# PEER expert stage: one gather of paired U and V rows (32 tokens x 4 slots), with streamed weight tables, in a hybrid decoder layer

## The chip, the cores and the metric

The kernel runs on one core of a Trainium2 chip. The metric is the device time of one execution in microseconds (us); lower is better. Before the change three runs gave 4285.42, 4292.56 and 4297.67 us, so the median is 4292.56 us.

## What is computed

One decoder layer over 1024 tokens of width 1024, all in float32. First two token mixers (a gated linear attention, GLA, and an RG-LRU) are computed from one projection, merged by gates, and projected by `w_out`. Then comes the PEER expert stage, the long part. For each token and each of 8 heads it picks 16 of 16384 experts through a product of two key sets, so each token has 128 expert slots:

```
qry = (xt @ w_query).reshape(T, 8, 2, 128)
sub_scores = einsum('thpd,hpnd->thpn', qry, sub_keys)      # 2 x 128 scores a head
top_s, top_i = top_k(sub_scores, 16)
cand_s, cand_i = all 256 sums of a pair of top_s, and their expert numbers
best_s, best_pos = top_k(cand_s, 16); gates = softmax(best_s)
u_sel = u_table[expert_idx]; v_sel = v_table[expert_idx]    # rows of 1024 floats, 4 KB
act = gelu(einsum('td,thkd->thk', xt, u_sel))
out = einsum('thk,thkd->td', gates * act, v_sel)
```

With 1024 tokens x 128 slots there are 131,072 rows of U and as many of V, 4 KB each: 1073.7 MB in all. Norms, modulation vectors and a residual stand around both halves of the layer.

## The kernel before

Three stages follow one another, each one block of five engine programs: `conditioning_and_lru`, `gated_linear_attention`, `peer_block`. SyncE (SP) issues most direct DMAs, GpSimd (POOL) issues the gathers, TensorE (PE) multiplies, VectorE (DVE) and ScalarE (ACT) do the rest. Engines meet at semaphores; each engine's queue is strictly in order.

In the LRU stage, ACT, PE, DVE, POOL and SP each run a loop of 8 blocks (`j`), in GLA a loop of 4 heads (`h`). SP loads 512 KB weight tiles a few steps ahead in both.

`peer_block` handles the tokens in 8 tiles of 128, one token in each partition. Before the first tile, 16 products of keys and query weights make the table `Wk` (8 MB, kept in SBUF, as is `w_out`, 4 MB). A tile has 8 heads, a head 2 groups `G` of `R = 8` slots. For a slot POOL issues one gather of 128 U rows (`gather_u`, L1010, 8 buffers `ur`) and one of 128 V rows (`gather_v`, L1015, 4 buffers `vr`), each 512 KB, alternating in `both`. At the head of a group POOL also copies the indices twice (L1003). DVE multiplies a U buffer with the tokens' h2 and sums to one number a token (`products`, L1323), then forms the group's 8 gelu-and-gate coefficients with one tanh on ACT (L1329 to L1334, L1071). ACT builds for each slot a 128x128 diagonal matrix of coefficients (L1075). PE multiplies it with the V buffer into the accumulator `ps_acc` (L1178: two products of 512 columns, each shown as two MATMUL rows). Selection of a head's experts (`select_sides`, `select_pairs`, L1279 to L1316) is written into the same DVE program two heads ahead, so that gathers start once two heads of tile 0 are selected. A gather waits until its buffer is free: U for DVE (`u_used`), V for PE (`v_used`).

Of the kernel before, what the change touches and what calls it, by code (L numbers as in the profile page):

```python
# [30 lines left out]
SLOTS = PH * TOPK  # L31
NEG = -3.0e38
# [33 lines left out]

def conditioning_and_lru(nc, ctx, keep, a, mod_dram, merged_dram):


    hh, hl, alow, ident = keep["hh"], keep["hl"], keep["alow"], keep["ident"]  # L70
    Q = 256
    CQ = Q // P
    MOD1 = 2 * D // Q
    with ExitStack() as scope:
# [140 lines left out]
        def _(act):  # L215
# [36 lines left out]
            with act.Fori(0, KC) as j:  # L252
                act.wait_ge(projected[0], j + 1)
# [210 lines left out]
def gated_linear_attention(nc, ctx, keep, a, merged_dram):  # L464
# [6 lines left out]
    with ExitStack() as scope:  # L471
        def sb(name, shape, dt=F32):
            return scope.enter_context(nc.sbuf_tensor(name, shape, dt))

        def sem(name):
            return ctx.enter_context(nc.semaphore(name))
# [135 lines left out]

# [164 lines left out]
        def _(dve):  # L777
# [84 lines left out]
            step.end(HEADS)  # L862


def peer_block(nc, ctx, keep, a, mod_dram, merged_dram, out):
# [4 lines left out]
    R = 8  # L870
    GROUPS = TOPK // R
    VR = ND = 4
    with ExitStack() as scope:
# [11 lines left out]
        Wk = sb("Wk", [P, KC, 2 * PH * NK])  # L885
        w_out = sb("w_out", [P, KC, D])
        mod = sb("mod", [P, 4 * D])
        mT = sb("mT", [P, KC, P])
        x2n, x2c = sb("x2n", [P, D]), sb("x2c", [P, D])
        h2n, h2c = sb("h2n", [P, D]), sb("h2c", [P, D])  # L890
        h2T = sb("h2T", [P, KC, P])
        yf = sb("yf", [P, D])
        ur, vr = sb("ur", [P, R, D]), sb("vr", [P, VR, D])
        diag = sb("diag", [P, ND, P])
        zero = sb("zero", [P, P], mybir.dt.bfloat16)
        idx = sb("idx", [P, 2 * SLOTS], U32)
        gates = sb("gates", [P, 2 * SLOTS])
        uidx, vidx = sb("uidx", [P, 2, R], U32), sb("vidx", [P, 2, R], U32)
# [21 lines left out]
        const, small_in = sem("consts3"), sem("small_in3")  # L920
        wout_in = [sem("wout_in0"), sem("wout_in1")]
        wq_in = [sem(f"wq_in{i}") for i in range(4)]
        wk_done, wk_out = sem("wk_done"), sem("wk_out")
        mod_ready = sem("mod_ready")
        x_in, m_in = sem("x_in3"), sem("m_in")
        y_done, y_sq, y_root, y_rstd, y_used = sem("y_done"), sem("y_sq"), sem("y_root"), sem("y_rstd"), sem("y_used")
        x2_ready, h2_ready, h2_turned, h2T_out = sem("x2_ready"), sem("h2_ready"), sem("h2_turned"), sem("h2T_out")
        x2_copied, h2_copied = sem("x2_copied"), sem("h2_copied")
        sc_done, sc_used = sem("sc_done"), sem("sc_used")
        negm_ready, ex_out, sel_ready = sem("negm_ready"), sem("ex_out"), sem("sel_ready")  # L930
        ucopy, vcopy, pool_go = sem("ucopy"), sem("vcopy"), keep["go"]
        u_in = [sem(f"u_in{r}") for r in range(R)]
        v_in = [sem(f"v_in{r}") for r in range(VR)]
        u_used, v_used = sem("u_used"), sem("v_used")
        gel_ready, tanh_out, coef_ready, diag_out = sem("gel_ready"), sem("tanh_out"), sem("coef_ready"), sem("diag_out")
        acc_done, acc_out, f_root, f_rstd, f_ready, out_done = (sem(n) for n in ("acc_done", "acc_out", "f_root", "f_rstd", "f_ready", "out_done"))
        dve_step, dve_go = sem("dve_step3"), keep["go"]
# [4 lines left out]

        def group_at(G):

            return bass.ds(G % (2 * SLOTS // R) * R, R)

        @block.sync
        def _(sp):
            def load_keys(g, i):

                sp.dma_start(vr[:, i], a["wqT"][g].rearrange("o p d -> (o p) d")).then_inc(wq_in[i], 16)
                sp.dma_start(diag[:, i], a["keysT"][g].rearrange("o p d -> (o p) d")).then_inc(wq_in[i], 16)

            def merged_tile(t):
                sp.dma_start(mT[:], merged_dram[:, :, bass.ds(t * P, P)]).then_inc(m_in, 16)

            def x_tile(t):
                sp.dma_start(x2n[:], a["x"][bass.ds(t, 1)].rearrange("o p d -> (o p) d")).then_inc(x_in, 16)

            def store_tile(t):  # L960
                sp.wait_ge(f_ready, t + 1)
                sp.dma_start(out[bass.ds(t, 1)].rearrange("o p d -> (o p) d"), yf[:]).then_inc(out_done, 16)

            for s in range(2):
                load_keys(slice(s, s + 1), s)
            merged_tile(0)
            for s in range(2):
                sp.dma_start(w_out[:, :, s * HALF:(s + 1) * HALF], a["w_out"][:, :, s * HALF:(s + 1) * HALF]).then_inc(wout_in[s], 16)
            x_tile(0)
            sp.dma_start(mod[:], mod_dram).then_inc(small_in, 16)  # L970

            for i, n in enumerate(("gain_post_mix", "gain_pre_ffn", "gain_post_ffn")):
                sp.dma_start(ur[:, 2 + i], a[n].broadcast_to([P, D])).then_inc(small_in, 16)
            for i in range(2, 4):
                load_keys(slice(i, i + 1), i)
            with sp.Fori(0, PH // 2 - 1) as g:
                for i in range(4):
                    sp.wait_ge(wk_done, 4 * g + i + 1)
                    load_keys(bass.ds(4 * g + i + 4, 1), i)
            sp.wait_ge(y_done, 2)  # L980
            merged_tile(1)
# [12 lines left out]
        @block.gpsimd
        def _(pool):
            nc.gpsimd.memset(eps[:], EPS).then_inc(const, 1)
            nc.gpsimd.memset(zero[:], 0.0).then_inc(const, 1)
            nc.gpsimd.iota(iota[:], [[1, TOPK]], base=0, channel_multiplier=0, allow_small_or_imprecise_dtypes=True).then_inc(const, 1)

            def copy_indices(G, par, to, copied):  # L1000

                pool.sem_inc(pool_go, 1)
                nc.gpsimd.tensor_copy(to[:, par], idx[:, group_at(G)]).then_inc(copied, 1)  # L1003
                pool.wait_ge(copied, G + 1)

            def gather_u(G, par, r, first=False):
                if not first:
                    pool.wait_ge(u_used, R * (G - 1) + r + 1)  # L1008
                pool.sem_inc(pool_go, 1)
                pool.indirect_dma_start(ur[:, r], None, a["u"], bass.IndirectOffsetOnAxis(ap=uidx[:, par, r:r + 1], axis=0)).then_inc(u_in[r], 16)  # L1010

            def gather_v(G, par, r):
                pool.wait_ge(v_used, R * G + r + 1)
                pool.sem_inc(pool_go, 1)
                pool.indirect_dma_start(vr[:, r % VR], None, a["v"], bass.IndirectOffsetOnAxis(ap=vidx[:, par, r:r + 1], axis=0)).then_inc(v_in[r % VR], 16)  # L1015

            def both(G, par):

                copy_indices(G + 1, 1 - par, uidx, ucopy)
                copy_indices(G, par, vidx, vcopy)  # L1020
                for r in range(R):
                    gather_u(G + 1, 1 - par, r)
                    gather_v(G, par, r)

            pool.wait_ge(mod_ready, 1)
            pool.wait_ge(sel_ready, 1)
            copy_indices(0, 0, uidx, ucopy)
            for r in range(R):
                gather_u(0, 0, r, first=True)
            pool.wait_ge(wk_done, 2 * PH)  # L1030
            with pool.Fori(0, TC * PH - 1) as H:
                both(2 * H, 0)
                pool.wait_ge(sel_ready, H + 2)
                both(2 * H + 1, 1)
            last = 2 * TC * PH - 1
            both(last - 1, 0)
            copy_indices(last, 1, vidx, vcopy)
            for r in range(R):
                gather_v(last, 1, r)

        @block.scalar
        def _(act):
            S = nc.scalar
            act.wait_ge(const, 3)
            act.sem_inc(diag_out, R)

            def mixer_norm(t, stored):
                act.wait_ge(y_done, 2 * t + 2)
                if stored is not None:
# [11 lines left out]
            def tile_turned(t):  # L1061
# [3 lines left out]
            def select_gates(n):  # L1065
                act.wait_ge(negm_ready, n + 1)
# [75 lines left out]
        def _(pe):  # L1142
# [61 lines left out]
            for h in range(2):  # L1204
                scores(h, 0, h)
# [257 lines left out]
```

## Time and profile before

| | |
|---|---|
| median of 3 runs | 4292.56 us |
| span of the profiled execution, first to last instruction | 4370.2 us |
| PE, DVE, ACT, POOL busy | 76%, 58%, 22%, 61% |
| DMA moved | 1184.53 MB, mean 271 GB/s |
| software queue (POOL's gathers above all) | 1084.36 MB |

The profile gives the profiled execution's time as its span alone; it is 77.6 us above the median of the unprofiled runs. Busy shares are averages over three unlike stages: the mixers take about the first 926 us, the expert stage the rest. "DMA share" is the mean busy share of the core's 16 DMA engines.

### The profile page before, as it was taken

How to read it: one execution, taken by the hardware profiler on the slowest of the kernel's cores; microseconds unless marked ns; L12 is line 12 of the kernel's file. 1: busy time of each engine (PE TensorE's matmuls, PEld its weight loads, DVE VectorE, ACT ScalarE, POOL GpSimd, SP SyncE). 2: the span in 40 equal slices, each digit the busy share in tenths (PEclk: the TensorE clock that was granted, in tenths of full speed). 3: DMA queues.
4: the chain of work that ended last, by engine and by line, in shares of the span. 5: the costliest groups of instructions: out<-in, count | busy, mean ns of one | idle time of the engine just before them, and what ended most of it. 6: DMA issues, size and time to landing. Idle time of an engine off the chain costs nothing.

```text
span 4370.2 us, 44073 instructions
## 1 busy us (share of the span) xinstructions
PE 3333.3 (76%) x9929; PEld 1731.2 (40%) x9944; DVE 2548.4 (58%) x5725; ACT 961.4 (22%) x1993; POOL 2665.9 (61%) x2467
## 2 busy tenths in 40 slices
PE   6998999977777767777677677767777677777676
PEld 5775888854222322232233222323332233222232
DVE  5786656635555565556655655565556556555654
ACT  4232444432111111112111111111111111111111
POOL 2233322205777677767776777777777767777776
PEclk9999999989999999999999999999999999999998
DMA  4323111138889898989989999999998889898998
GB/s 178 133 100 116 43 58 58 38 135 288 320 320 329 318 327 317 331 315 327 323 318 325 326 331 322 326 326 339 317 330 318 314 320 330 319 324 319 332 339 293
DMA packets 334937, 1184.53 MB, mean 271 GB/s; under 512 B 36944, under 2 KB 51728, under 8 KB 330640
## 3 DMA queue, kind: packets, MB, share of 16 engines
q0 software_dynamic: 297984, 1084.36, 69.2%
q1 hardware_dynamic: 36880, 99.45, 6.3%
q14 instruction: 58, 0.48, 0.0%
q8 instruction: 15, 0.25, 0.0%
HBM read 1168.98 MB, written 14.68 MB: 271 GB/s over the span
## 4 chain that ended last, share of the span: by engine, by line
issue 23%; DMA 19%; POOL 19%; PE 14%; DVE 2%; POOLq 1%; ACT 1%; another core or an unknown queue 0%; SPq 0%; DVEq 0%; ACTq 0%
DMA vr<-in_v,vidx 16%; PE ps_acc L1178 10%; POOL vr L1015 9%; POOL ur L1010 8%; DMA ur<-in_u,uidx 2%; PE ps_y L1149 2%; PE ps_sc L1164 2%; DVE ur L1323 1%; POOL vidx L1003 1%; POOL uidx L1003 1%; DMA ur<-in_gain_post_ffn 0%; POOLq L1003 0%; PE ps_acc L1194 0%; POOLq L1008 0%
## 5 line engine op out<-in xcount | busy, mean ns | idle before, releaser
L1178 PE MATMUL ps_acc<-vr,diag 128*128 128x512 f32 x4096 | 2095.4, 642 | 888.8 <-DMA vr<-in_v,vidx 712.5
L1178 PEld LDWEIGHTS ps_acc<-vr,diag 128*128 128x128 f32 x4096 | 742.3, 199 | 2215.2 <-issue 1766.6
L1323 DVE SCALAR_TENSOR_TENSOR ur<-ur,h2c 128x1024 f32<-128x1024 f32 x1024 | 1205.5, 1223 | 497.5 <-DMA ur<-in_u,uidx 465.0
L1015 POOL DMA_INDIRECT vr<-in_v,vidx x1024 | 1138.1, 1111 | 487.2 <-issue 301.1
L1010 POOL DMA_INDIRECT ur<-in_u,uidx x1024 | 1148.5, 1122 | 401.2 <-issue 260.5
L1075 ACT ACTIVATE diag<-ident,coef 128x128 f32<-128x128 f32 x1024 | 370.8, 396 | 1486.8 <-PE ps_acc L1178 703.9
L1315 DVE RECIPROCAL esum<-esum 128x1 f32<-128x1 f32 x64 | 10.5, 163 | 588.1 <-ACT ex L1067 404.3
L1071 ACT ACTIVATE gel<-gel 128x8 f32<-128x8 f32 x128 | 26.6, 208 | 1139.8 <-DVE gel L1330 985.8
L1164 PE MATMUL ps_sc<-Wk,h2T 128*128 (+1 forms) x1024 | 245.7, 395 | 15.4 <-ACT h2T L1063 10.8
L1164 PEld LDWEIGHTS ps_sc<-Wk,h2T 128*128 128x128 f32 x1024 | 203.1, 200 | 71.3 <-issue 42.8
L589 POOL CAST wh<-wt 128x1024 fp32r<-128x1024 f32 x32 | 38.2, 1192 | 304.2 <-PE ps_b L64 161.7
L62 PE MATMUL ps_b<-hh,wh 128*128 128x512 f32 x320 | 132.7, 415 | 2.6 <-POOL wl L591 2.6
L831 DVE TENSOR_TENSOR sm<-ps_s,masks 128x1024 f32<-128x1024 f32 x32 | 39.2, 1224 | 156.2 <-PE ps_s L734 156.2
L63 PE MATMUL ps_b<-hl,wh 128*128 128x512 f32 x320 | 128.2, 401 | 0.0
L64 PE MATMUL ps_b<-hh,wl 128*128 128x512 f32 x320 | 128.1, 400 | 0.0
L1003 POOL COPY uidx<-idx 128x8 uint32 (+1 forms) x128 | 70.5, 551 | 80.2 <-DVEq L1317 61.0
L1149 PE MATMUL ps_y<-w_out,mT 128*128 (+1 forms) x256 | 114.0, 599 | 2.4 <-DMA w_out<-in_w_out 2.4
L1003 POOL COPY vidx<-idx 128x8 uint32 (+1 forms) x128 | 72.8, 569 | 28.7 <-POOL uidx L1003 17.8
L591 POOL TENSOR_TENSOR wl<-wt,wh 128x1024 fp32r<-128x1024 f32 x32 | 82.4, 2575 | 2.6
L1323 DVE DVE_READ_ACCUMULATOR ur<-ur,h2c 128x1 f32 x1024 | 83.5, 82 | 0.0
L189 POOL CAST wh<-wt 128x1024 fp32r<-128x1024 f32 x27 | 30.4, 1124 | 81.4 <-issue 52.4
L1279 DVE MAX8 top<-ps_sc 128x8 f32<-128x128 f32 x128 | 38.4, 300 | 67.5 <-PE ps_sc L1164 44.5
(272 smaller groups left out, 3895.0 us busy)
## 6 DMA issues: line engine op xcount, KB each, us to landing
ada<-in_w_ada SPq DMA_DIRECT2D x24, 1024.0 KB, 5.5
wt<-in_w_head SPq DMA_DIRECT2D x32, 512.0 KB, 3.5
ur<-in_u,uidx POOLq DMA_INDIRECT x1024
vr<-in_v,vidx POOLq DMA_INDIRECT x1024
wt<-in_w_lru SPq DMA_DIRECT2D x27, 512.0 KB, 9.2
vr<-in_wqT SPq DMA_DIRECT2D x16, 512.0 KB, 5.3
xt<-in_x POOLq DMA_DIRECT2D x8, 512.0 KB, 5.1
merged_scratch<-lru POOLq DMA_DIRECT2D x8, 512.0 KB, 2.9
```

The source lines that it names most:

```text
L62: nc.tensor.matmul(out, wh, xh, start=first, stop=False)
L63: nc.tensor.matmul(out, wh, xl, start=False, stop=False)
L64: return nc.tensor.matmul(out, wl, xh, start=False, stop=last)
L591: g.tensor_tensor(wl[:, i % 4], wt[:, i % 2], wh[:, i % 4], ALU.subtract).then_inc(w_split, 1)
L1003: nc.gpsimd.tensor_copy(to[:, par], idx[:, group_at(G)]).then_inc(copied, 1)
L1010: pool.indirect_dma_start(ur[:, r], None, a["u"], bass.IndirectOffsetOnAxis(ap=uidx[:, par, r:r + 1], axis=0)).then_inc(u_in[r], 16)
L1015: pool.indirect_dma_start(vr[:, r % VR], None, a["v"], bass.IndirectOffsetOnAxis(ap=vidx[:, par, r:r + 1], axis=0)).then_inc(v_in[r % VR], 16)
L1075: S.activation(diag[:, r % ND], ident[:], ACT.Copy, scale=coef[:, par, r:r + 1]).then_inc(diag_out, 1)
L1149: last = nc.tensor.matmul(ps_y[:, bass.ds(s * HALF, HALF)], mT[:, k], w_out[:, k, bass.ds(s * HALF, HALF)], start=(k == 0), stop=(k == KC ...
L1164: last = nc.tensor.matmul(ps_sc[:, 0:2 * NK], h2T[:, k], Wk[:, k, bass.ds(h * 2 * NK, 2 * NK)], start=(k == 0), stop=(k == KC - 1))
L1178: last = nc.tensor.matmul(ps_acc[:, half(s)], diag[:, r % ND], vr[:, r % VR, half(s)], start=False, stop=False, skip_group_check=True)
L1323: last = v.scalar_tensor_tensor(ur[:, r], ur[:, r], 1.0, h2c[:], ALU.mult, ALU.mult, accum_out=dots[:, r:r + 1])
```

## The change

During the mixers, 64 DMAs of 2 MB on ACT's queue copy U and V from DRAM into one DRAM table `uv`, in which the U row and the V row of an expert stand side by side (8 KB). In `peer_block` one gather fetches, for 32 tokens and 4 slots, 128 such rows into one of 12 buffers of 8 KB a partition; partition 32s+i holds token 32b+i, slot s of the round. So a round is 4 gathers (b = 0 to 3) for 128 tokens x 4 slots, and a tile has 32 rounds. h2 has to be spread in the same way: it is stored to DRAM and read back four times a tile (`h2r`). DVE sums dot products as before; ACT makes four 128x32 matrices `stack` (a mask times a coefficient) in place of four 128x128 diagonals; PE multiplies each with the V half of a buffer into 32 partitions of `ps_acc`. Indices and gates are spread over the partitions by 16 small ACT copies for each half tile. `Wk` and `w_out` no longer stay in SBUF: `Wk` goes to DRAM, and 12 blocks of 1 MB a tile (4 of `w_out`, 8 of `Wk`) stream through 3 buffers. Tile 0 is selected whole before its products begin; the selection of tile t+1 is spread over the rounds of tile t. Loops are unrolled. The GLA stage frees its semaphores and a barrier follows it.

```diff
+def interleave_experts(act, keep, a, chunk):
+    rows = bass.ds(chunk * UV_ROWS, UV_ROWS)
+    act.dma_start(keep["uv"][rows, 0, :], a["u"][rows, :]).then_inc(keep["uv_copied"], 16)
+    act.dma_start(keep["uv"][rows, 1, :], a["v"][rows, :]).then_inc(keep["uv_copied"], 16)
...
             with act.Fori(0, KC) as j:
+                for i in range(2):
+                    interleave_experts(act, keep, a, 2 * j + i)
                 act.wait_ge(projected[0], j + 1)
...
             with act.Fori(0, HEADS) as h:
+                for i in range(4):
+                    interleave_experts(act, keep, a, 4 * h + (2 * KC + i))
                 act.wait_ge(z_done, h + 1)
...
+    nc.clear_and_free_semaphores(own)
+    nc.all_engine_barrier()
...
-    R = 8
-    VR = ND = 4
+    NR = 12
+    ROUNDS = SLOTS // 4
+    WB, Q = 3, 256
...
+            def load_block(t, i):
+                n = BLOCKS * t + i
+                if n >= WB:
+                    sp.wait_ge(wb_used, n - WB + 1)
...
+            def spread_rows(t):
+                sp.wait_ge(h2_stored, 16 * (t + 1))
...
+                for s in range(4):
+                    sp.dma_start(h2r[32 * s:32 * s + 32, t % 2], h2_dram[t].rearrange("(b i) d -> i b d", b=4)).then_inc(h2r_in[t % 2], 16)
...
+            def gather(R, b):
+                t, r, n = R // ROUNDS, R % ROUNDS, 4 * R + b
+                if b == 0 and r % (ROUNDS // 2) == 0:
+                    pool.wait_ge(uidx_ready, R // (ROUNDS // 2) + 1)
+                if n >= NR:
+                    pool.wait_ge(v_used, (n - NR) // 4 + 1)
+                pool.indirect_dma_start(uv[:, n % NR], None, keep["uv"].rearrange("e w d -> e (w d)"), bass.IndirectOffsetOnAxis(ap=uidx[:, t % 2, b, r:r + 1], axis=0)).then_inc(uv_in[n % NR], 16)
+            pool.wait_ge(key_done, KEYS)
+            pool.wait_ge(keep["uv_copied"], 32 * UV_CHUNKS)
...
+            def stacks(R):
+                act.wait_ge(coef_ready, R + 1)
...
+                for b in range(4):
+                    S.activation(stack[:, R % 2, b], mask[:], ACT.Copy, scale=coef[:, R % 2, b:b + 1]).then_inc(stack_out, 1)
...
+            def mix(R):
...
                 for s in range(2):
+                    for b in range(4):
+                        last = nc.tensor.matmul(ps_acc[32 * b:32 * b + 32, half(s)], stack[:, R % 2, b], uv[:, (4 * R + b) % NR, D + s * HALF:D + (s + 1) * HALF], start=(r == 0), stop=(r == ROUNDS - 1), skip_group_check=True)
+                last.then_inc(v_used, 1)
...
+            for r in range(2, ROUNDS):
+                next_tile(0, r)
+            for t in range(TC):
+                for r in range(ROUNDS):
+                    products(t, r)
+                    coefficients(t, r)
...
+                    if t + 1 < TC:
+                        next_tile(t + 1, r)
```

## Rows read from the trace of the kernel before

**Rows 1.** The page: span, and the 40 slices' DMA share and rate.
```profile
span 4370.2 us, 44073 instructions
...
DMA  4323111138889898989989999999998889898998
GB/s 178 133 100 116 43 58 58 38 135 288 320 320 329 318 327 317 331 315 327 323 318 325 326 331 322 326 326 339 317 330 318 314 320 330 319 324 319 332 339 293
...
q0 software_dynamic: 297984, 1084.36, 69.2%
```
**Rows 2.** The page: chain of waits by line; costliest groups (busy, mean ns, idle).
```profile
DMA vr<-in_v,vidx 16%; PE ps_acc L1178 10%; POOL vr L1015 9%; POOL ur L1010 8%; DMA ur<-in_u,uidx 2%; PE ps_y L1149 2%; PE ps_sc L1164 2%; DVE ur L1323 1%; POOL vidx L1003 1%; POOL uidx L1003 1%; DMA ur<-in_gain_post_ffn 0%; POOLq L1003 0%; PE ps_acc L1194 0%; POOLq L1008 0%
...
L1178 PE MATMUL ps_acc<-vr,diag 128*128 128x512 f32 x4096 | 2095.4, 642 | 888.8 <-DMA vr<-in_v,vidx 712.5
...
L1323 DVE SCALAR_TENSOR_TENSOR ur<-ur,h2c 128x1024 f32<-128x1024 f32 x1024 | 1205.5, 1223 | 497.5 <-DMA ur<-in_u,uidx 465.0
```
**Rows 3.** Stages: us, busy by engine, granted clock, DMA share, GB/s.
```profile
109.00:437.00 328.00, 294.12 (x1189) 220.00 (x1188) 244.06 (x249) 96.44 (x89) 99.11 (x75) 0.97 0.31 116
437.00:926.00 489.00, 475.23 (x2711) 411.68 (x2709) 289.98 (x314) 231.42 (x377) 112.54 (x60) 0.98 0.13 46
1100.00:4300.00 3200.00, 2314.13 (x5142) 943.09 (x5155) 1859.24 (x4817) 539.97 (x1383) 2328.10 (x2205) 0.96 0.90 324
```
**Rows 4.** Stretches of 20 and 10 us in the expert stage, same columns.
```profile
2000.00:2020.00 20.00, 15.20 (x28) 5.24 (x28) 7.42 (x29) 4.47 (x12) 13.37 (x15) 0.91 0.98 375
2020.00:2040.00 20.00, 13.74 (x32) 7.11 (x33) 17.89 (x44) 2.08 (x7) 14.21 (x13) 0.83 0.81 263
...
2160.00:2180.00 20.00, 13.98 (x30) 4.82 (x29) 10.34 (x30) 3.17 (x10) 15.03 (x16) 1.00 0.99 387
...
2260.00:2280.00 20.00, 13.75 (x30) 4.74 (x28) 7.50 (x27) 3.89 (x12) 13.19 (x15) 1.00 0.99 370
...
1060.00:1070.00 10.00, 7.14 (x16) 2.52 (x15) 0.81 (x2) 0.80 (x2) 6.06 (x7) 1.00 1.01 401
```
**Rows 5.** Timeline at 1056 and 2019 us: start, us, engine, [idle before].
```profile
1056.73 0.95 POOL L1010 DMA_INDIRECT ur<-in_u,uidx  x1 [0.30 <-issue]
1057.98 0.94 POOL L1015 DMA_INDIRECT vr<-in_v,vidx  x1 [0.30 <-issue]
...
1058.53 1.96 PE L1178 MATMUL ps_acc<-vr,diag 128*128 128x512 f32 x4 [0.80 <-DMA vr<-in_v,vidx]
...
2019.00 0.16 DVE L1315 RECIPROCAL esum<-esum 128x1 f32<-128x1 f32 x1 [10.57 <-ACT ex L1067]
```
**Rows 6.** Timeline: one head selected on DVE, two products, ACT's small tanh.
```profile
976.05 0.30 DVE L1279 MAX8 top<-ps_sc 128x8 f32<-128x128 f32 x1 [9.27 <-PE ps_sc L1164]
...
987.40 0.23 DVE L1316 TENSOR_SCALAR gates<-ex,esum 128x16 f32<-128x16 f32 x1
...
1026.56 1.22 DVE L1323 SCALAR_TENSOR_TENSOR ur<-ur,h2c 128x1024 f32<-128x1024 f32 x1
...
1027.70 1.22 DVE L1323 SCALAR_TENSOR_TENSOR ur<-ur,h2c 128x1024 f32<-128x1024 f32 x1
...
1029.38 0.21 ACT L1071 ACTIVATE gel<-gel 128x8 f32<-128x8 f32 x1 [9.20 <-DVE gel L1330]
```
**Rows 7.** Timeline, 926 to 1018 us: SP's loads, DVE, ACT's last key copy.
```profile
929.06 4.08 SPq L968 DMA_DIRECT2D w_out<-in_w_out  x2
933.18 3.84 SPq L958 DMA_DIRECT2D x2n<-in_x  x1
...
939.64 0.64 SPq L951 DMA_DIRECT2D vr<-in_wqT  x1
...
958.43 1.22 DVE L1245 TENSOR_TENSOR mod<-mod,ur 128x1024 f32<-128x1024 f32 x1
...
1017.57 1.02 ACT L1105 ACTIVATE Wk<-ps_acc 128x1024 f32 x1 [0.76 <-PE ps_acc L1194]
```
**Rows 8.** ACT before the first wait of an LRU block and of a head.
```profile
254.89 1.03 ACT L255 ACTIVATE arena<-ps_xl 128x1024 f32<-128x1024 f32 x1 [6.86 <-PE ps_xl L64]
...
559.72 1.28 ACT L616 ACT_TABLE_LOAD   x1 [7.92 <-DVE hp L784]
```
**Rows 9.** The U gathers; their first and last start.
```profile
L1010 POOL DMA_INDIRECT ur<-in_u,uidx x1024: 941/946/1999, 989.0 to 4334.5; - x171
```

More of the change, by code:

```diff
@@ L941, in peer_block @@
         wk_banks = (ps_h, ps_acc)
-        def group_at(G):
-            return bass.ds(G % (2 * SLOTS // R) * R, R)
+        key_rows = lambda i: (uv[:, i, 0:D], uv[:, i, D:D + NK])
+        wk_stage = lambda h: uv[:, KL + h % KL]
         @block.sync
         def _(sp):
[L949 to L969, printed above, removed]
@@ L1025, in _ @@
-            pool.wait_ge(mod_ready, 1)
[L1026 to L1037, printed above, removed]
@@ new lines, in _ @@
+            act.wait_ge(mod_ready, 1)
+            for g in range(2):
+                key_columns(g)
+            mixer_norm(0)
+            for g in range(2, 4):
+                key_columns(g)
+            expert_norm(0)
+            for g in range(4, KEYS):
+                key_columns(g)
+            for r in range(5, ROUNDS):
+                next_tile(0, r)
+            for t in range(TC):
+                for r in range(ROUNDS):
+                    R = ROUNDS * t + r
+                    if R > 0:
+                        stacks(R - 1)
+                    if r == 0 and t > 0:
+                        finish(t - 1)
+                    if t + 1 < TC:
+                        next_tile(t + 1, r)
+                    tanh(R)
@@ L1139, in _ @@
+            stacks(ROUNDS * TC - 1)
             finish(TC - 1)
@@ L1226, in _ @@
-            pe.wait_ge(acc_out, TC - 1)
-            edge(True)
-            with pe.Fori(0, PH - 2) as h:
-                scores(PH * (TC - 1) + h + 2, TC - 1, h + 2)
-                head(PH * (TC - 1) + h)
-            for H in range(PH * TC - 2, PH * TC):
-                head(H)
-            edge(False).then_inc(acc_done, 1)
+                    last = nc.tensor.matmul(ps_sc[:, 0:2 * NK], h2T[:, k], wb[:, n % WB, k], start=(k == 0), stop=(k == KC - 1))
+                last.then_inc(wb_used, 1)
@@ new lines, in next_tile @@
+            def next_tile(t, r):
+                if r < 2:
+                    mixed(t, 2 * r)
+                    mixed(t, 2 * r + 1)
+                if r == 4:
+                    turn(t)
+                if r >= 6 and r % 3 == 0 and r < 30:
+                    scores(t, r // 3 - 2)
+            mixed(0, 0)
+            mixed(0, 1)
+            for g in range(2):
+                keys(g)
+            mixed(0, 2)
+            mixed(0, 3)
+            for g in range(2, KEYS):
+                keys(g)
@@ new lines, in select_experts, with indices, products @@
+                dve.wait_ge(sel_ready, PH * t + h + 1)
+            def indices(t, m):
+                dve.wait_ge(spread_out, 2 * t + m + 1)
+                rounds = slice(m * ROUNDS // 2, (m + 1) * ROUNDS // 2)
+                if t >= 2:
+                    dve.wait_ge(v_used, ROUNDS * (t - 1))
+                v.tensor_copy(uidx[:, t % 2, :, rounds], spread[:, t % 2, 0, :, rounds]).then_inc(uidx_ready, 1)
+            def products(t, r):
+                R = ROUNDS * t + r
+                if r == 0:
+                    dve.wait_ge(h2r_in[t % 2], 64 * (t // 2 + 1))
+                for b in range(4):
+                    n = 4 * R + b
+                    dve.wait_ge(uv_in[n % NR], 16 * (n // NR + 1))
+                    v.scalar_tensor_tensor(uv[:, n % NR, 0:D], uv[:, n % NR, 0:D], 1.0, h2r[:, t % 2, b], ALU.mult, ALU.mult, accum_out=dots[:, R % 2, b:b + 1]).then_inc(dots_done, 1)
@@ L1383, in _, with next_tile @@
-            step.end(TC - 1)
-            with dve.Fori(0, PH - 2) as h:
-                step.loop(h, HEAD_STEPS)
-                head(PH * (TC - 1) + h)
-            step.end(PH - 2)
-            for H in range(PH * TC - 2, PH * TC):
-                head(H, select=False, more=H < PH * TC - 1)
+            def next_tile(t, r):
+                if r == 2:
+                    mixer_norm(t)
+                if r == 3:
+                    expert_norm(t)
+                if r >= 7 and r % 3 == 1 and r < 31:
+                    select_sides(t, r // 3 - 2)
+                if r >= 8 and r % 3 == 2:
+                    select_pairs(t, r // 3 - 2)
+                if r >= 9 and r % 3 == 0:
+                    select_experts(t, r // 3 - 3)
+                if r == 19:
+                    indices(t, 0)
+                if r == 31:
+                    indices(t, 1)
```

537 lines of the change are left out of this document (262 added, 275 removed).

## The prediction

> **What bounds the kernel now.** I read the page's slices first, then the stretches by stage, the chain of waits and the costliest groups, and last short timelines of POOL, DVE and ACT.
>
> The slices show two regimes [rows 1]. Up to slice 8 the DMA engines are busy 10 to 40% of the time, and from slice 9 on 80 to 90%, at 314 to 339 GB/s in the slices between the first and the last. The stretches say what each part waits for [rows 3]. In the mixers PE is busy 294 of 328 us and 475 of 489 us while the DMA share is 0.31 and 0.13: PE sets the pace and DMA stands idle. In the expert stage no compute engine is full over 3200 us (PE 72%, DVE 58%, POOL 73%); the DMA share is 0.90 and the rate 324 GB/s. The chain of waits agrees [rows 2]: landing V rows 16%, the two gathers' issue on POOL 9% and 8%, PE's own product only 10%. PE idles 712.5 us and DVE 465 us for gathers [rows 2].
>
> So the stage is bound by the flow of gathered rows, and this flow has gaps. Where the queues are full, stretches of 20 us show shares of 0.98 to 0.99 and 370 to 387 GB/s, and a stretch of 10 us 401 [rows 4]. Right beside them stands 263 GB/s at 0.81. Two reasons for gaps can be read. POOL needs 0.94 + 0.30 us for each gather of 512 KB, so two gathers (1 MB) take 2.5 us of POOL, 419 GB/s at the very best [rows 5]: it can't catch up after a stall. And the stalls come from the order of work: at 2019 us DVE has waited 10.57 us for ACT's exp, which stood in ACT's queue behind diagonals that waited for V rows [rows 5]. Meanwhile no U buffer came free.
>
> **The bytes.** A tile needs 128 gathers of 1.049 MB = 134.2 MB, as before. New are 12 table blocks of 1.049 MB (12.6 MB), four reads of spread h2 (2.1 MB) and six transfers of 0.524 MB for x, mixer output, x2 and h2 out, x2 back, output (3.1 MB): 17.8 MB a tile, of which all but x, mixer output and output (1.6 MB) is new. These streams are no longer free, since the DMA engines are the resource that is short. With tile 0's prepared ahead and its first 12 gathers taken off, what is left to stream is 1073.7 - 12.6 + 7 x 17.8 = 1186 MB.
>
> **The rate.** One POOL instruction now brings 1.049 MB, so POOL needs 1.25 us where DMA needs about 2.7: its ceiling goes. Twelve buffers of 1 MB replace 12 of 0.5 MB, so up to 12.6 MB are in flight, over 30 us of transfers. A buffer is freed after DVE's last product (1.15 us), coefficients (about 1.4 us), stacks (1 us) and PE's 8 products. Two V products cost 1.96 us now [rows 5], so 8 cost at most 7.8 us at this clock: some 12 us, under the 21 us that the two following rounds keep DMA busy. So the queue should seldom run dry. What a full queue delivers has bounds. Low: while its packets were under way, the software queue moved 1084.36 MB in 0.692 x 4370.2 us = 358.6 GB/s [rows 1]. High: 401 GB/s [rows 4]. The three full 20 us stretches average 377 at 0.987, or 382 at 1.00 [rows 4]. I take 390, nearer to these rows than to the ends: 8 KB rows halve the descriptors and the semaphore writes. 1186 MB / 390 = 3041 us.
>
> What a page says against this: the Trainium skill, "DMA: Bandwidth & Descriptors", section "Where 436 GB/s comes from", states that transfers between HBM and SBUF are bound by the HBM side at about 358 GB/s a core. By that rule streaming would take 1186 / 358 = 3313 us and the change would lose; the trace does not agree over short stretches (387 and 401 GB/s [rows 4]), but its mean while busy does.
>
> **The mixers.** 134.2 MB are copied where the DMA share was 0.31 and 0.13 [rows 3]. At 390 GB/s the copies need 344 us of DMA, spread over 817 us; both stages stay under about 0.85 even at half that rate. ACT issues 4 a block and 8 a head. SP's issues beside other loads took 0.64 us for 128 rows, and 2 us and 3.84 us where `w_out`'s many short rows stood in the queue [rows 7]. ACT idles 6.86 us before an LRU block's first work and 7.92 us before a head's [rows 8]. At 0.64 us an issue the 4 cost 2.6 us and the 8 cost 5.1 us, both hidden; at 3.84 us they would stick out by 8.5 us x 8 and 22.8 us x 4, some 155 us. The queue is empty when ACT begins, so the short issue is the nearer row. I take 15 us in all, with the added barrier and slower weight loads; bounds 0 and 155.
>
> **The start of the expert stage.** Before, gathers run from 989 us [rows 9], after two heads. After the change:
> - GLA ends at 926 + 15 = 941. The modulation is ready at 959.65 now [rows 7], 34 us after 926; so at 975. ACT's key copies now wait for it.
> - 16 key products, limited by ACT's copies, SP's loads and h2's store: now 16 end at 1018.6 [rows 7], 59 us after the modulation, but two heads' scores and their selection stand between them. I take 38 us: 1013. Then the turn of h2, the store and reload of a `Wk` block, and scores: two transfers of 1.049 MB at 2.7 us and some 7 us of PE and ACT, 13 us: 1026.
> - A head's selection on DVE takes 987.63 - 976.05 = 11.6 us [rows 6]. Four heads, the fifth's first part, and the spread of indices on ACT (16 copies, of about the 0.21 us of its small tanh [rows 6]): 1026 + 46 + 9 = 1081, first gathers. Three rounds fill the 12 buffers by about 1115, and then DMA idles.
> - All eight heads and the second spread: 1026 + 93 + 5 = 1124, first products. One round through DVE (4 x 1.14 us, the spacing of two products [rows 6]), ACT and PE: 1140, first buffer free. From here the stream runs.
>
> **The rest.** DVE has per tile 32 x (4.6 + 1.4) + 8 x 11.6 + about 9 for norms and finish = 294 us, ACT less, against 152 MB / 390 = 390 us for DMA: hidden. Rounds with selection have 10 us on DVE of 12 us. In each tile's first round ACT's finish and PE's wait for `acc_out` (some 8 us) stand in the chain; the full buffers cover most, I take 2 us x 7. After the last gather: products, coefficients, PE and the final norm and store, 20 us.
>
> **Sum**, against the profiled span: 1140 + 3041 + 14 + 20 = 4215 us, where before it was 4370.2. The median of the runs is 77.6 us under the span, a ratio of 0.982, which I keep: 4215 x 0.982 = 4140 us, 3.5% faster. The margin is thin at one place: with everything else the same, the new span equals the old at 1186 / (4370 - 1174) = 371 GB/s.
>
> **Rivals.**
> 1. *The full queue isn't faster than the mean while busy.* For it: 358.6 GB/s is an average over all 1024 MB, and the full stretches are chosen. Against: stretches at share 0.98 and more were all 370 to 387. It decides below 371 GB/s. At 358.6, 3307 us of streaming, span 4481, time 4400: slower by 2.5%, since some 115 MB more go through the same engines and the start is 150 us later. Chance 0.17.
> 2. *DVE or PE becomes the bound.* If each round's tanh sits 4 us behind other work of ACT, DVE needs 294 + 128 = 422 us a tile: 1124 + 7 x 422 + 344 + 20 = 4442, time 4363. For PE: its granted clock fell to a mean of 0.83 to 0.91 in stretches with waits [rows 4], and a round's products in one burst leave it idle between. At half the clock a round would need 15.7 us; but then PE no longer idles, which should lift the clock. Against both: DVE's 75% of the new pace. Chance 0.06.
> 3. *The copies collide with the mixers.* At the upper bound, 155 us late instead of 15: span 4355, time 4277, no change or a little faster. For it: 16.8 MB in one burst at each head. Against: 7 us of idle time and a DMA share of 0.13. Chance 0.05.
> 4. *The row goes as two transfers of 4 KB.* Then POOL's instruction takes up to twice as long, still under DMA's 2.7 us, and the rate is 382: 3105 us, time 4203. This lies inside the forecast.
>
> **The numbers.** Forecast (with 4) 0.72, rival 1 0.17, rival 2 0.06, rival 3 0.05. A change under 0.3%, 13 us, can't be told from none. Faster 0.73, the same 0.06, slower 0.21. Range: 410 GB/s without the 15 and 14 us gives span 1125 + 2892 + 20 = 4037, time 3965; 365 GB/s gives 1140 + 3249 + 34 = 4423, time 4344, and part of rival 3 on top. I give 3980 to 4370; rival 1 in full lies just outside.
>
> **What would show it.** Right: in the stage from 1150 us on a DMA share of 0.97 or more in nearly all slices and 380 to 400 GB/s; POOL's gathers waiting for `v_used`, not for issue; about 26 us for two rounds; mixers' end under 945 us; first products at about 1124. Wrong: a share of 1.0 at 360 GB/s (rival 1); slices at 0.8 with DVE or PE at over 90% (rival 2); GLA ending after 1000 us (rival 3); first products much after 1150.

## The result, and the profile after

The changed kernel took 4226.38 us (median of 4 runs, 4225.8 to 4232.22) where the kernel before took 4295.11 us (4285.42 to 4300.59): a ratio of 0.9845, 95% interval 0.9826 to 0.9863. It is faster by 1.55%, which is small but clear of the noise of this comparison. The forecast was 4140 us and 3.5% faster: the sign held and the time lies in the range, but less than half of the forecast gain was measured. In a second comparison, described below, the same two kernels gave 4220.77 and 4373.04 us, a ratio of 0.9644 (0.959 to 0.9697), close to the forecast 0.9645. So the first question is why two comparisons differ, and the second is which terms of the sum were right.

The page of the changed kernel, its slices, queues and chain:

```profile
span 4224.4 us, 34179 instructions
...
PE 2183.7 (52%) x10168; PEld 1228.1 (29%) x10168; DVE 2603.5 (62%) x6254; ACT 883.7 (21%) x2334; POOL 1404.9 (33%) x1186
...
DMA  6999634624569999999999999999999999999997
GB/s 219 303 316 306 221 97 142 199 84 135 202 259 362 421 415 403 389 419 415 375 421 416 416 379 420 414 377 411 417 416 367 421 414 399 393 421 421 422 419 322
...
q0 software_dynamic: 150528, 1084.30, 63.0%
q1 hardware_dynamic: 86512, 233.67, 15.2%
q10 hardware_dynamic: 33792, 134.22, 10.8%
...
DMA uv<-uv_scratch,uidx 41%; PE ps_acc L1253 7%; POOL uv L1082 7%; DMA wb<-in_w_out 4%; DVE uv L1373 2%; ACT stack L1143 2%; PE ps_y L1215 2%; DMA uv<-in_keysT 0%; DVE coef L1385 0%; DVE gel L1380 0%; DVE gel L1379 0%; PE ps_h L1205 0%; DMA h_scratch<-h2n 0%; SPq L979 0%; ACT spread L1134 0%
```

Against [rows 1] the late slices are full: 9 tenths from slice 12 to the last but one, and up to 422 GB/s. The chain is now 41% landing gathers where V rows had 16% [rows 2]. But the high slices begin at 12 or 13 (counted from 0) instead of 9. Stretches (us, busy of PE, PEld, DVE, ACT, POOL, granted clock, DMA share, GB/s):

```profile
437.00:926.00 489.00, 377.12 (x2050) 321.33 (x2050) 199.30 (x234) 176.74 (x285) 99.84 (x58) 0.86 0.48 146
926.00:1094.00 168.00, 122.97 (x679) 106.43 (x678) 70.36 (x83) 58.93 (x95) 14.51 (x9) 0.85 0.42 131
1094.00:1246.00 152.00, 87.39 (x412) 74.51 (x413) 51.04 (x182) 28.05 (x49) 0.20 (x2) 0.72 0.72 256
1246.00:1296.00 50.00, 28.78 (x95) 20.94 (x95) 42.14 (x152) 6.85 (x29) 11.44 (x13) 0.76 0.99 378
1296.00:4190.00 2894.00, 1188.21 (x5400) 423.05 (x5398) 1929.41 (x5238) 470.84 (x1720) 1161.81 (x1012) 0.66 1.01 407
```

The mixers, which ended at 926 us, now end at 1094, with PE busy 377 of 489 us where it was busy 475 [rows 3]. From 1296 us the DMA engines move 407 GB/s over 2894 us, against 324 before [rows 3]. The loss in the mixers can be read on ACT's queue at the start of a head; the last row is part of the first work of the head there:

```profile
603.86 0.55 ACTq L71 DMA_DIRECT2D uv_scratch<-in_u  x1
604.62 0.53 ACTq L72 DMA_DIRECT2D uv_scratch<-in_v  x1
605.40 0.53 ACTq L71 DMA_DIRECT2D uv_scratch<-in_u  x1
606.14 3.51 ACTq L72 DMA_DIRECT2D uv_scratch<-in_v  x1
609.91 11.02 ACTq L71 DMA_DIRECT2D uv_scratch<-in_u  x1
621.14 12.69 ACTq L72 DMA_DIRECT2D uv_scratch<-in_v  x1
634.08 6.84 ACTq L71 DMA_DIRECT2D uv_scratch<-in_u  x1
641.14 8.66 ACTq L72 DMA_DIRECT2D uv_scratch<-in_v  x1
651.26 1.11 ACT L632 ACTIVATE oT<-ps_a,hp 128x1024 f32<-128x1024 f32 x1
```

Who waited for it from 437 to 1200 us (total, times, longest, in us):

```profile
DVE oT L804 <- ACT oT L632: 157.9, 4, 41.4
PE ps_a L63 <- DVE oT L804: 132.9, 4, 34.5
```

Three issues cost 0.53 to 0.55 us, the next five 3.5 to 12.7 us. The reading, which e2 and e3 test, is that the queue is then full and each further issue waits until earlier copies have drained. ACT is held for 46 us in this head. PE waits for it four times, 33 us in the mean.

That this wait sets the pace of GLA shows in the stage as a whole, before and after, with the same 2728 MATMUL rows:

```profile
424.00:926.00 502.00, 483.79 (x2728) 416.72 (x2728) 292.12 (x316) 236.13 (x380) 120.45 (x66) 0.97 0.15 51
442.00:1094.00 652.00, 500.09 (x2728) 427.77 (x2728) 269.66 (x316) 235.67 (x380) 114.35 (x66) 0.86 0.46 143
```

GLA takes 150 us longer: 133 us are PE's wait for ACT, and 16 us more PE is busy with the same rows, at a granted clock of 0.86 instead of 0.97. The other 18 us of the 168 arise in the LRU stage, which ends at 442 instead of 424 us.

### The profile page after: what moved, and what is told of

Same layout as the page of the kernel before. It is cut to its first block, busy times and chain, and to the rows that moved or that the text cites. A ratio compares the mean times of both kernels' runs of the same rounds, so it can differ in the third digit from the quotient of the medians.

```text
span 4224.4 us, 34179 instructions
## 1 busy us (share of the span) xinstructions
PE 2183.7 (52%) x10168; PEld 1228.1 (29%) x10168; DVE 2603.5 (62%) x6254; ACT 883.7 (21%) x2334; POOL 1404.9 (33%) x1186
## 3 DMA queue, kind: packets, MB, share of 16 engines
q10 hardware_dynamic: 33792, 134.22, 10.8%
## 4 chain that ended last, share of the span: by engine, by line
DMA 45%; PE 10%; POOL 7%; DVE 5%; issue 4%; ACT 2%; SPq 0%; ACTq 0%; POOLq 0%; DVEq 0%; PEldq 0%
DMA uv<-uv_scratch,uidx 41%; PE ps_acc L1253 7%; POOL uv L1082 7%; DMA wb<-in_w_out 4%; DVE uv L1373 2%; ACT stack L1143 2%; PE ps_y L1215 2%; DMA uv<-in_keysT 0%; DVE coef L1385 0%; DVE gel L1380 0%; DVE gel L1379 0%; PE ps_h L1205 0%; DMA h_scratch<-h2n 0%; SPq L979 0%; ACT spread L1134 0%
## 5 line engine op out<-in xcount | busy, mean ns | idle before, releaser
L1082 POOL DMA_INDIRECT uv<-uv_scratch,uidx x1024 | 1173.3, 1146 | 1921.6 <-PE ps_acc L1253 1534.8
L1373 DVE SCALAR_TENSOR_TENSOR uv<-uv,h2r 128x1024 f32<-128x1024 f32 x1024 | 1233.4, 1224 | 765.9 <-DMA uv<-uv_scratch,uidx 755.2
L1253 PE MATMUL ps_acc<-uv,stack 128*32 128x512 f32 x4096 | 857.4, 983 | 1617.4 <-ACT stack L1143 1614.5
L1253 PEld LDWEIGHTS ps_acc<-uv,stack 128*32 128x32 f32 x4096 | 146.6, 151 | 2235.1 <-ACT stack L1143 1921.3
L1236 PE MATMUL ps_sc<-wb,h2T 128*128 128x256 f32 x1024 | 279.0, 432 | 34.7 <-DVEq L1329 28.4
L1236 PEld LDWEIGHTS ps_sc<-wb,h2T 128*128 128x128 f32 x1024 | 219.5, 221 | 160.1 <-issue 126.1
L1143 ACT ACTIVATE stack<-mask,coef 128x32 f32<-128x32 f32 x1024 | 245.0, 310 | 73.9 <-DVE coef L1385 73.9
L1215 PE MATMUL ps_y<-wb,mT 128*128 128x256 f32 x512 | 138.0, 433 | 142.7 <-DMA wb<-in_w_out 142.7
L1215 PEld LDWEIGHTS ps_y<-wb,mT 128*128 128x128 f32 x512 | 110.7, 221 | 179.8 <-DMA wb<-in_w_out 146.3
L63 PE MATMUL ps_a<-hh,wh 128*128 128x512 f32 x64 | 29.9, 467 | 132.9 <-DVE oT L804 132.9
L1373 DVE DVE_READ_ACCUMULATOR uv<-uv,h2r 128x1 f32 x1024 | 83.9, 82 | 0.0
## 6 DMA issues: line engine op xcount, KB each, us to landing
wb<-in_w_out SPq DMA_DIRECT2D x32, 1024.0 KB, 26.1
h2r<-h_scratch SPq DMA_DIRECT2D x32, 512.0 KB, 16.5
```

Source lines behind the costliest of these rows:

```text
L63: nc.tensor.matmul(out, wh, xh, start=first, stop=False)
L1082: pool.indirect_dma_start(uv[:, n % NR], None, keep["uv"].rearrange("e w d -> e (w d)"), bass.IndirectOffsetOnAxis(ap=uidx[:, t % 2, b, r: ...
L1143: S.activation(stack[:, R % 2, b], mask[:], ACT.Copy, scale=coef[:, R % 2, b:b + 1]).then_inc(stack_out, 1)
L1215: last = nc.tensor.matmul(ps_y[:, c * Q:(c + 1) * Q], mT[:, k], wb[:, n % WB, k], start=(k == 0), stop=(k == KC - 1))
L1236: last = nc.tensor.matmul(ps_sc[:, 0:2 * NK], h2T[:, k], wb[:, n % WB, k], start=(k == 0), stop=(k == KC - 1))
L1253: last = nc.tensor.matmul(ps_acc[32 * b:32 * b + 32, half(s)], stack[:, R % 2, b], uv[:, (4 * R + b) % NR, D + s * HALF:D + (s + 1) * HALF ...
```

## The experiments

All start from the changed kernel unless said otherwise. e1 to e4 ran on one chip, e5 to e8 on a second and e9 on a third; each group has its own runs of the kernel before. e1, e3, e7, e8 and e9 are single runs, the others medians of four.

**The kernel before, once more.**

> The kernel before, unchanged, profiled once more. The forecast turned a span into a time by 4292.56 / 4370.2 = 0.982. If that ratio belongs to the kernel (profiling slows its many small gathers), the span is again 70 to 80 us above the unprofiled time of about 4295. If it belonged to that one profiled execution, span and time agree within 5 us, as they do in the changed kernel (4224.4 and 4226.0).

Measured: 4398.34 us for an execution whose span is 4396.3 us; the kernel before took 4374.76 us here (median of 7 runs, 4367.6 to 4386.55). Span and time of one execution agree within 2.1 us. So the 0.982 isn't a cost of profiling.

**The copies issued apart.** The same 64 copies, at other places of ACT's program:

```diff
-for i in range(2):
-    interleave_experts(act, keep, a, 2 * j + i)
 ...
 S.activation(xlp[:, 3:3 + T], ps_xl[:], ACT.Copy).then_inc(xl_out, 1)
+interleave_part(act, keep, a, 2 * j, 0)
+interleave_part(act, keep, a, 2 * j, 1)
 ...
 S.activation(xg, ps_xg[:], ACT.Copy).then_inc(xg_out, 1)
+interleave_part(act, keep, a, 2 * j + 1, 0)
+interleave_part(act, keep, a, 2 * j + 1, 1)
 ...
-for i in range(4):
-    interleave_experts(act, keep, a, 4 * h + (2 * KC + i))
 ...
 for c in range(TC): 
     if c < TC - 1:
         gate_half(c)
+    interleave_part(act, keep, a, 4 * h + (2 * KC + c // 2), c % 2)
```

> The same 64 copies of 2 MB, issued two at a time behind ACT's first two activations of an LRU block, and one in each of the 8 chunks of a GLA head, instead of 4 and 8 in a row. Theory A (ACT is held in issuing while its queue is full, and PE waits for ACT's first work of the head): issues take 0.5 to 0.6 us, the expert stage begins near 940 us instead of 1094, time about 4080. Theory B (the copies take the DMA engines from the weight loads): the bytes are the same, the expert stage begins within 30 us of 1094, time above 4190.

Measured: 4071.1 us against 4374.76, ratio 0.9297 (0.9274 to 0.9319). The timeline of ACT's queue in a head and of POOL at the start of the expert stage:

```profile
613.08 0.55 ACTq L71 DMA_DIRECT2D uv_scratch<-in_u  x1
621.18 0.53 ACTq L71 DMA_DIRECT2D uv_scratch<-in_v  x1
...
931.12 0.10 POOL L1073 MEMSET eps<- 128x1 f32 x1 [77.66 <-POOLq L880]
```

The mixers' stretch in the same kernel:

```profile
437.00:926.00 489.00, 477.56 (x2724) 414.51 (x2722) 290.89 (x316) 235.93 (x380) 115.78 (x62) 0.99 0.65 183
```

The expert stage begins at 931 us instead of 1094: theory A. All 134 MB are still copied, in the same stages (a share of 0.65 in this stretch), and PE is busy 478 of 489 us, as before the change. So the bytes, issued one or two copies at a time, cost the mixers some 5 us (931 against 926).

This edit takes away the held queue and the bursts together. POOL's waits for the weight loads of the heads fall with it, from 117.3 us to the 51 us of the kernel before. In the changed kernel those waits stayed hidden: PE waits for ACT in GLA (132.9 us), and otherwise 11 us for one load, as in the kernel before. What a burst does when the queue does not hold ACT is in the next run.

**Fewer, longer rows in the copies.** Rows of 16 KB on both sides, so U and V rows do not stand side by side:

```diff
+    part = bass.ds(chunk * 2 * UV_ROWS + w * UV_ROWS, UV_ROWS)
+    act.dma_start(keep["uv"].rearrange("e w d -> (e w) d")[part, :].rearrange("(r q) d -> r (q d)", q=4), a["u" if w == 0 else "v"][rows, :].rearrange("(r q) d -> r (q d)", q=4))...
```

> The same bytes in the same 64 issues at the same places, but as rows of 16 KB that are contiguous on both sides, so a quarter of the rows; U and V rows do not stand side by side then, and the gathered values are other ones. If a queue is full by the number of rows it holds, the issues no longer wait and the expert stage begins near 950 us, time about 4085. If it is full by bytes, or if the bytes themselves disturb the mixers, it begins near 1090 as now, time about 4225.

Measured: 4183.58 us, neither, and the expert stage begins between the two expected times:

```profile
1046.13 0.10 POOL L1074 MEMSET eps<- 128x1 f32 x1 [72.11 <-POOLq L881]
```

The queue of the copies on the page (packets, MB, share):

```profile
q10 hardware_dynamic: 3072, 134.22, 9.0%
```

One head's issues:

```profile
631.53 0.55 ACTq L73 DMA_DIRECT2D uv_scratch<-in_u  x1
632.30 0.53 ACTq L73 DMA_DIRECT2D uv_scratch<-in_v  x1
...
637.11 0.53 ACTq L73 DMA_DIRECT2D uv_scratch<-in_v  x1
```

And who waited on POOL:

```profile
POOL wh L605 <- DMA wt<-in_w_head: 224.4, 6, 57.7
...
POOL wh L200 <- DMA wt<-in_w_lru: 118.1, 7, 24.6
```

All eight issues take 0.53 to 0.55 us although the bytes are the same: the queue is full by a number of rows or packets, not of bytes (which of the two, no run parts). But now the weight loads of the mixers come late (224.4 and 118.1 us of waits on POOL, where the changed kernel has 117.3 and 49.4). 134.22 MB in 3072 packets, of which 64 x 16 can only be the completions, means data packets of 64 KB, and eight copies of 2 MB now stand in the queue at once. PE's one long wait in GLA, 40.3 us, goes back to a late load too: DVE waits 63.9 us for `masks` there. Whether these loads are late for the one or for the other wasn't tried. So a burst has two costs here: the held queue came first and hid the late loads, and with the first gone the second keeps the stage at 1046 us, 120 later than before the change.

**Without the paired table.** Two gathers for each buffer, no copies:

```diff
+for w, table in enumerate((a["u"], a["v"])):
+    pool.indirect_dma_start(uv[:, n % NR, w * D:(w + 1) * D], None, table, ...).then_inc(uv_in[n % NR], 16)
```

> No copies and no paired table: two gathers of 4 KB rows, one from U and one from V, fill each of the 12 buffers (2048 gathers of 512 KB); all else as in the changed kernel. The mixers end at 926 us again, 162 us earlier. Theory C (the rate in the expert stage rose because more is in flight and the order of work no longer empties the queue): the stage's rate stays at 395 GB/s or more and the time falls to about 4065 to 4090. Theory D (the 8 KB rows raised it, by POOL's halved issue and fewer rows): the rate is 370 GB/s or less, the time 4220 to 4300.

Measured: 4205.38 us against 4374.76, ratio 0.9608 (0.9584 to 0.9632). Between the two theories: the stretch runs at 388 GB/s at a share of 1.01.

```profile
1142.00:4181.00 3039.00, 1225.27 (x5424) 437.48 (x5424) 1941.85 (x5249) 472.40 (x1725) 2239.10 (x2024) 0.65 1.01 388
```

Of the 83 GB/s gained over 324 [rows 3], 64 came without the paired rows and 19 with them. What the 19 are isn't shown: the pairing gives wider rows and halves POOL's instructions, and POOL is nearly full here. In this stretch it waited for:

```profile
POOL uv L1072 <- issue: 591.7, 1940, 0.5
POOL uv L1072 <- PE ps_acc L1242: 162.8, 41, 35.3
```

Its 2239 us busy and these 592 us between gathers make 93% of 3039 us, and it waits only 163 us for freed buffers, so the 12 buffers are seldom all in flight. The share of 1.01 speaks for the rows, this for POOL. Compared with the kernel that issues its copies apart, on the same chip, the paired table is worth 4205.38 - 4071.1 = 134 us, once its copies hold nobody up.

**The changed kernel again, beside other runs of the kernel before.**

> The changed kernel, unchanged, timed beside the kernel before, on whatever chip this is. The kernel before took 4295 us in one comparison and 4375 us in another; the changed one 4226 us in the first. If a chip shifts both alike, the ratio stays at 0.985 (0.983 to 0.986). If the chip shifts only the kernel before, whose queue runs empty again and again, the changed kernel stays within 10 us of 4226 whatever the other does: 0.966 where that takes 4375.

Measured: 4220.77 us (4213.18 to 4226.83) against 4373.04 (4353.56 to 4393.76), ratio 0.9644 (0.959 to 0.9697). The changed kernel stayed within 6 us; the kernel before moved by 78. In four comparisons it took 4295, 4375, 4373 and, in one run, 4267 us. The last three ran on three chips; the chip of the first isn't recorded. Whether it is the chip, and what in it, was not tried.

**w_out in 8 KB rows**, on top of the copies issued apart:

```diff
-sp.dma_start(wb[:, n % WB], a["w_out"][:, :, i * Q:(i + 1) * Q])
+sp.dma_start(wb[:, n % WB], a["w_out"][i])      # host layout [4, P, KC, 256]
```

> e2 (spread issue) with w_out's four blocks laid out so that a block is 128 rows of 8 KB instead of 1024 rows of 1 KB. In each tile of the changed kernel PE waits about 18 us for a w_out block, which lands 26 us after its issue where a Wk block of the same size, 8 KB rows, lands after 9 us; POOL and then the gathers stop behind it. Theory E (each engine takes a row of each queue in turn, so small rows get a small share): blocks land in about 10 us, PE's wait for w_out falls from 143 to under 50 us, the stage's rate rises from 406 to 412 GB/s or more, time 4071 - 50 = about 4020. Theory F (the loads are late because SP issues them late): landing stays above 20 us and the time within 10 us of 4071.

Measured: 4054.89 us against 4373.04, ratio 0.9269 (0.9218 to 0.932). The DMA issues with their median time to landing (us), in the changed kernel:

```profile
wb<-wk_scratch SPq DMA_DIRECT2D x64, 1024.0 KB, 9.4
wb<-in_w_out SPq DMA_DIRECT2D x32, 1024.0 KB, 26.1
```

In e6, and then PE's wait for these blocks there:

```profile
wb<-wk_scratch SPq DMA_DIRECT2D x64, 1024.0 KB, 9.8
wb<-in_w_out SPq DMA_DIRECT2D x32, 1024.0 KB, 9.1
```
```profile
PE ps_y L1215 <- DMA wb<-in_w_out: 33.6, 8, 19.8
```

Theory F is refuted, and the landing fits theory E: same bytes, 26.1 to 9.1 us, and PE's waits shrink to 33.6 us (from 142.9 us in e2). Turns between queues are not shown apart from a price of short rows by themselves. The time gained is 16 us, not the expected 50, between two chips that time the kernel before alike (4374.76 and 4373.04): the rate over 1400 to 3900 us only goes from 406 to 408. The full buffers must have covered most of the wait. The Trainium skill, "DMA: Bandwidth & Descriptors", section "Queues, rings and completion order", says that each DMA engine takes the queues with work in turn, a packet at a time; the two landings agree with it, no more.

**Eight buffers instead of twelve**, with the paired table, and without it:

```diff
+    NB = 8
...
-                if n >= NR:
-                    pool.wait_ge(v_used, (n - NR) // 4 + 1)
+                if n >= NB:
+                    pool.wait_ge(v_used, (n - NB) // 4 + 1)
```

> The changed kernel with gathers in a ring of 8 of its 12 buffers: 8.4 MB in flight instead of 12.6 MB, the same 8 KB rows and the same order of work. If depth is what keeps the queue full, two rounds are too few: one round (10.5 us of DMA) has to cover products, coefficients, stacks, PE and selection, and the stage falls to 330 to 370 GB/s, time 4400 to 4700. If it is the order of work and the wider rows, it stays above 400 GB/s, time within 40 us of 4226.

> e4 (two gathers of 4 KB rows a buffer, no copies) with 8 of the 12 buffers: about the depth of the kernel before (8.4 against 6.3 MB in flight), the same rows as there, but the changed order of work. If depth matters most: 320 to 350 GB/s, time 4500 or more. If order does: 380 GB/s or more, within 50 us of e4's 4205.

Measured: 4442.56 us with the table, 4439.34 us without. The stretch from 1400 to 3900 us in e7, then in e8:

```profile
1400.00:3900.00 2500.00, 1003.50 (x4441) 371.36 (x4439) 1598.45 (x4393) 384.99 (x1394) 919.22 (x800) 0.65 0.97 380
```
```profile
1400.00:3900.00 2500.00, 962.07 (x4225) 355.19 (x4224) 1514.58 (x4143) 371.82 (x1338) 1660.44 (x1522) 0.64 0.97 361
```

By time, depth matters most: 222 us in the one (against 4220.77), 234 in the other (against e4's 4205.38, on another chip), and both end above the kernel before's 4373. By rate the first case lost less than its theory said (380 against 406, forecast 330 to 370); the second lost 29 of 390 and lies between its two theories. Even then, at 8.4 MB in flight, e8 keeps 361 GB/s with the kernel before's 4 KB rows where that kernel has 324 with 6.3 MB: the rest is the order of work and the last step of depth, which no run parts.

**Fewer bytes in the streamed tables**, on e6, with `w_out`'s blocks cut in the same way:

```diff
+cols = KC * Q if t < 2 else Q
+sp.dma_start(wb[:, n % WB].rearrange("p k n -> p (k n)")[:, 0:cols], wk_dram[i - QUARTERS][:, 0:cols])...
...
```

> e6 with the table blocks of tiles 2 to 7 cut to an eighth of their columns, so that 6 x 12 x 0.918 MB = 66 MB less is moved; the scores and the mixer output of these tiles are computed with stale tables, all instructions stay. If the expert stage is bound by bytes, it shortens by 66 MB / 408 GB/s = 162 us, from 4055 to about 3893. If the gathers' own latency or DVE's order bounds it, by less than 50 us.

Measured: 3910.39 us, 144 us less than e6's 4054.89, for 66 MB: 2.2 us a MB, where a rate of 408 GB/s gives 2.45. The stretch still runs full, 405 GB/s at 1.01:

```profile
1400.00:3700.00 2300.00, 1002.07 (x4608) 360.30 (x4608) 1650.65 (x4521) 407.66 (x1476) 996.97 (x846) 0.67 1.01 405
```

So the stage is bound by the bytes moved, and the streamed tables, which replace 12 MB of SBUF by traffic, are paid for in full: at this price the 12.6 MB of seven tiles cost some 190 us. (This and e6 ran on different chips. The kernel before took 4267 us beside this run and 4373 beside e6; the changed kernel moved by 6 us between its two comparisons.)

## Why the prediction was right or wrong

The sum, term by term, in the span of the profiled execution (POOL's and DVE's rows give the starts):

| term | forecast | measured |
|---|---|---|
| expert stage begins | 941 | 1094 |
| from there to the first gather | 140 | 152 |
| from there to the first products | 183 | 193 |
| stream restarts (first buffer free) | 1140 | 1296 |
| stream, with tile edges | 3055 | 2912 |
| rest after it | 20 | 16 |
| span | 4215 | 4224 |
| span to time | -75 | +2 |

The start of the stage in the changed kernel's timeline, by these rows of POOL and DVE:

```profile
1094.18 0.10 POOL L1073 MEMSET eps<- 128x1 f32 x1 [76.06 <-POOLq L880]
...
1246.07 1.02 POOL L1082 DMA_INDIRECT uv<-uv_scratch,uidx  x1 [151.70 <-DVE uidx L1364]
...
1287.16 1.22 DVE L1373 SCALAR_TENSOR_TENSOR uv<-uv,h2r 128x1024 f32<-128x1024 f32 x1
...
1295.99 0.97 POOL L1082 DMA_INDIRECT uv<-uv_scratch,uidx  x1 [35.14 <-PE ps_acc L1253]
```

*Failed: "a ratio of 0.982, which I keep".* This step alone puts the time 75 us off. I took the gap between the profiled span and the median for a property of the kernel. In e1 span and time of one execution agree within 2.1 us, and in the changed kernel they do as well (4224.4 and 4226.0). The kernel before takes 4267 to 4375 us from comparison to comparison, so the span of 4370.2 fits the slower ones and the 4295 us of the first a faster one. Which chip that profile came from isn't recorded, so this last step is an inference. By its own frame, 4215 / 4370, the forecast ratio was 0.9645; e5 measured 0.9644.

That agreement is luck and must not be read as a confirmed sum. Two terms were wrong, 153 us too little and 143 us too much, and cancelled:

*Failed: "I take 15 us in all" for the mixers.* It was 168. I had both bounds, 0 and 155 (its terms, 8 x 8.5 and 4 x 22.8 us, make 159), and chose near the low one because "the queue is empty when ACT begins". It is empty for the first three issues; a head's 8 issues are 4096 rows, and from the fourth on ACT waits for room (in an LRU block, four issues, from 3.3 to 13.5 us at the fourth). The rows for `w_out` [rows 7] had hinted at this: 3.84 us for an issue behind its two loads of 1024 rows each. I priced each issue by itself, and never counted rows against what the queue had been seen to take. So rival 3, given 0.05, is what happened in the mixers: its sign, GLA ending after 1000 us, its place, the burst at each head, and nearly its price. It did not say what would wait; the trace says ACT, and e2 moves the same bytes and begins the expert stage at 931 us.

*Mis-sized, and without harm in e2: the copies' own rate*, priced at 390 GB/s. In GLA the spread copies of e2 add 137 GB/s and 0.52 of DMA share to what the kernel before has, some 263 GB/s while busy. The DMA share in the LRU stage is 0.93 in the changed kernel and 0.94 in e2, not under 0.85; at half of 390 GB/s the stage's 67 MB alone take 344 us of its 328, so "even at half that rate" didn't follow from its own numbers.

*Mis-sized: the rate, "I take 390".* It was 407 over 2894 us, and the stream 143 us shorter. In full stretches of 20 us it is higher still, above the best row of before (the middle row is another matter, see the last section):

```profile
2180.00:2200.00 20.00, 6.87 (x32) 1.16 (x32) 15.41 (x46) 2.12 (x9) 6.17 (x6) 0.62 1.01 421
2080.00:2100.00 20.00, 3.64 (x16) 0.59 (x16) 5.50 (x12) 1.96 (x6) 4.35 (x5) 0.50 1.02 317
2220.00:2240.00 20.00, 6.94 (x33) 1.26 (x33) 15.59 (x49) 2.72 (x12) 7.77 (x7) 0.51 1.02 423
```

I scaled 377 GB/s at a share of 0.987 to 1.00 and added 2% for the wider rows. But a stretch at 0.99 in a kernel whose queue empties every few rounds isn't a full queue, and its rate isn't the ceiling; 401 over 10 us [rows 4] was nearer. e4 to e8 show what moves the rate: with direct 4 KB rows and 12 buffers it is 388 to 390, with paired rows 406, and with 8 buffers 361 and 380.

*Right: what bounds the stage.* The share is 1.01 from 1296 us on, and e9's 66 MB less bring 144 us. POOL no longer paces: it waits 1534.8 us for freed buffers, as forecast, and DVE's 755.2 us of idle time are for gathers. *Right: the start*, each of its marks within 12 us of the forecast distance from the stage's begin.

*Rival 1*, the rate staying at 358.6 GB/s, is refuted: the trace has 407 over 2894 us. It does not agree either with the rule of about 358 GB/s a core that the Trainium skill, "DMA: Bandwidth & Descriptors", section "Where 436 GB/s comes from", gives for HBM to SBUF. The Trainium skill, "HBM Reference", section "Specifications (TRN2)", says that a core that streams alone measures about 425; 421 and 423 over 20 us here are close to that. *Rival 2* is refuted for PE and DVE: DVE is busy 1929 of 2894 us. PE's busy share fell to 41% and its granted clock to 0.66 in the mean, and the DMA share stayed at 1.01. *Rival 4*, two transfers of 4 KB a row, didn't happen: POOL's gather has a median of 946 ns as before [rows 9], and its queue went from 297984 packets [rows 1] to 150528. 131072 of these are the rows, one packet each; two a row would be 262144.

## What to carry to other kernels

Count the rows that a burst of DMAs puts in its queue, not only the bytes and the price of one issue: the engine that issues stands still once the queue is full, and everything behind it in its order with it. Here the same 134 MB cost 168 us from two loops' heads and some 5 when issued one or two at a time. A remedy for the held engine alone isn't enough: with fewer, longer rows the burst still cost 120 us, now by late loads. In a stage bound by gathers, first deepen what is in flight (8 to 12 buffers was worth over 220 us), then widen the rows, and price each streamed table at the full rate. And time both kernels in more than one comparison, on more than one chip, before the size of a gain of 2% is believed.

## What the runs showed of the hardware that was not expected

- The issuing engine held by a full queue: 0.53 to 0.55 us an issue for the first three DMAs of 512 rows, then 3.5 to 12.7 us each. With rows of 16 KB, packets of 64 KB, all eight took 0.53 to 0.55 us (e3), and then the mixers' loads landed late instead.
- Eight products of 128x32 by 512 columns, 16 MATMUL rows, in 1.92 us in this row of the changed kernel; before, two products of 128x128 (4 rows) took 1.96 us [rows 5]:

```profile
2057.53 1.92 PE L1253 MATMUL ps_acc<-uv,stack 128*32 128x512 f32 x16 [0.44 <-PE ps_y L1215]
...
2193.46 3.64 PE L1253 MATMUL ps_acc<-uv,stack 128*32 128x512 f32 x16 [9.20 <-ACT stack L1143]
```

 I had forecast up to 7.8 us for them. That four products into different groups of 32 columns run at once is what the Trainium skill, "TensorEngine Tiling (Array Packing)", section "Key Properties", states of such tiles; the 1.92 us agree. The granted clock is 1.00 around the first row. Around the second, after a wait of 9.20 us, it is 0.50, the lower of the two levels, and the same 16 rows take 3.64 us. (The profile models the ends of MATMULs.)
- In the stretch from 2080 us above, the DMA engines are as busy as ever (1.02), but only 317 GB/s arrive. In it fall the four reads of spread h2, of which each writes into 32 partitions and which take 16.5 us to land. That they cause it wasn't tried.
- The kernel before varied from 4267 to 4375 us over four comparisons, the changed one only between 4221 and 4226 us in two. Whether the chip makes the difference, and why for the one kernel and not the other, stays open.
